# Recurrent core of a two-block kernel: where the first inverse products are put, and the order of the copies around them

## What is computed

```python
def step(state, inp):
    r_t, w_t, k_t, v_t, kk_t, a_t = inp
    sa = jnp.einsum('bhvk,bhk->bhv', state, kk_t)
    state = (state * w_t[:, :, None, :]
             - sa[..., :, None] * (kk_t * a_t)[..., None, :]
             + v_t[..., :, None] * k_t[..., None, :])
    return state, jnp.einsum('bhvk,bhk->bhv', state, r_t)
```

## Time and profile before

| | us |
|---|---|
| median of three executions | 2788.71 (2783.32 to 2795.54) |
| profiled execution, its time | 2797.66 |
| its span in the trace | 2795.9 |
| recurrent core, first copy of scores to last output product | 410.84 to 653.70 |
| PE busy in the whole span | 2590.9 (93%) |
| mean granted clock of TensorE | 0.954 |

### The profile page before, as it was taken

One profiled execution on the slowest core, in us unless ns is written; L12 is line 12 of the kernel. 1 busy time (PEld: TensorE's weight loads), 2 busy tenths in 40 slices (PEclk: granted clock), 3 DMA queues, 4 the chain that ended last, 5 costly groups with the idle time before them and its releaser, 6 DMA issues.

```text
span 2795.9 us, 35552 instructions
## 1 busy us (share of the span) xinstructions
PE 2590.9 (93%) x15475; PEld 1540.2 (55%) x15644; DVE 1138.2 (41%) x1288; ACT 561.5 (20%) x617; POOL 940.0 (34%) x390
## 2 busy tenths in 40 slices
PE   4869999999989999999998889999799999999996
PEld 1545558886445555555554556675345555555552
DVE  5466566663443220222224687355442220222233
ACT  3226431221121110011102323321231100111102
POOL 0212110000134444445545677201134443444450
PEclk7989999998989999999998999989899999999997
DMA  5432020000001111111113612300011111111101
GB/s 239 166 121 75 28 102 3 3 3 16 30 31 47 52 60 42 43 53 45 57 42 136 106 38 72 133 1 23 30 38 46 47 58 47 46 49 50 60 31 60
DMA packets 44267, 162.65 MB, mean 58 GB/s; under 512 B 4560, under 2 KB 14288, under 8 KB 41168
## 3 DMA queue, kind: packets, MB, share of 16 engines
q1 hardware_dynamic: 38496, 151.21, 16.3%
q10 hardware_dynamic: 5616, 9.17, 1.1%
HBM read 147.77 MB, written 12.58 MB: 57 GB/s over the span
## 4 chain that ended last, share of the span: by engine, by line
PE 86%; DVE 6%; issue 2%; DMA 2%; POOL 2%; ACT 1%; ACTq 0%; SPq 0%; DVEq 0%; POOLq 0%
PE pt L918 18%; PE pt L924 17%; PE pt L921 16%; PE pt L1233 11%; PE pt L561 7%; PE pt L411 3%; PE pt L700 2%; PE pt L1939 2%; PE pt L1945 2%; PE pt L1942 2%; PE pt L344 1%; DVE work L532 1%; DMA work<-in_xT 1%; PE pt L332 1%; PE pt L397 1%
## 5 line engine op out<-in xcount | busy, mean ns | idle before, releaser
L889 POOL TENSOR_TENSOR weights_rounded<-work,cst 128x1024 fp32r<-128x1024 f32 (+1 forms) x120 | 314.8, 2624 | 950.5 <-issue 683.8
L893 POOL TENSOR_TENSOR slots<-work,weights_rounded 128x1024 bf16<-128x1024 f32 (+1 forms) x120 | 346.3, 2885 | 9.4
L921 PE MATMUL pt<-work,weights_rounded 128*128 128x512 bf16 x1358 | 340.3, 382 | 2.8 <-issue 0.2
L561 PE MATMUL pt<-work 64*64 64x64 f32 (+5 forms) x4512 | 220.5, 250 | 13.4 <-DVE work L532 12.4
L921 PEld LDWEIGHTS pt<-work,weights_rounded 128*128 128x128 bf16 x1408 | 125.2, 99 | 182.2 <-issue 64.3
L561 PEld LDWEIGHTS pt<-work 64*64 64x64 f32 (+3 forms) x4512 | 202.2, 148 | 32.0 <-DVE work L532 17.3
L918 PE MATMUL pt<-rounded,weights_rounded 128*128 128x512 f32 x704 | 206.1, 428 | 8.8 <-DVE work L1859 5.2
L918 PE MATMUL pt<-rhs_rounded,weights_rounded 128*128 128x512 f32 x704 | 206.4, 429 | 7.8 <-DVE work L815 4.2
L918 PE MATMUL pt<-hidden_rounded,weights_rounded 128*128 128x512 f32 x704 | 207.5, 427 | 0.0
L1006 DVE SCALAR_TENSOR_TENSOR slots<-pt,par,slots 128x1023 f32<-128x1023 f32 x44 | 56.4, 1283 | 332.2 <-ACT slots L992 332.2
L924 PE MATMUL pt<-hidden_rounded,slots 128*128 128x512 bf16 x696 | 178.7, 387 | 1.0
(11 more groups left out here) (332 smaller groups left out, 3504.8 us busy)
## 6 DMA issues: line engine op xcount, KB each, us to landing
work<-in_w_up SPq DMA_DIRECT2D x88, 512.0 KB, 3.6
work<-in_w_mod SPq DMA_DIRECT2D x11, 2048.0 KB, 9.7
work<-in_w_down SPq DMA_DIRECT2D x32, 704.0 KB, 4.0
slots<-in_w_in SPq DMA_DIRECT2D x31, 512.0 KB, 4.1
slots<-in_w_v SPq DMA_DIRECT2D x10, 512.0 KB, 3.9
work<-in_xT ACTq DMA_DIRECT2D x4, 1024.0 KB, 22.8
x_scratch<-work SPq DMA_DIRECT2D x8, 512.0 KB, 2.7
slots<-in_w_out SPq DMA_DIRECT2D x8, 512.0 KB, 3.3
```

The source lines that it names most:

```text
L561: return pe.matmul(out, lhs, rhs, start=start, stop=stop, skip_group_check=True)
L889: did(pool, pool.tensor_tensor(w_hi(n, cols).rearrange("p (k n) -> p k n", n=P), w_raw(n, cols).rearrange("p (k n) -> p k n", n=P), const( ...
L893: did(pool, pool.tensor_tensor(w_lo(n, cols), w_raw(n, cols), w_hi(n, cols).bitcast(F32), ALU.subtract), "ffn_w_split")
L921: pe.matmul(out, top_half(w_hi(n, cols))[:, k * P:k * P + P], rhs_lo(k), start=False, stop=False, skip_group_check=True)
```

## The change

The first inverse products of pair `i` go to `PT[(i + 3) % 4]`: pair 0 to `PT[3]`, pair 1 to `PT[0]`, pair 2 to `PT[1]`. So they wait not for their own scores to be copied but for those of the pair before them, and those of pair 0 for none. `mv_kept` of the chunk before is now waited for ahead of them. DVE's order becomes: scores 0, scores 1, first inverse 0, scores 2, first inverse 1, first inverse 2. The mv products wait for first inverse 0 (their tile holds the products that it reads) and, pair by pair, for the copy of the scores. The X products of the first level wait one first inverse further, since their bank holds the products of the next pair. The order of the four quadrants in the first inverse products changes too. The number of instructions is the same.

```diff
+        def l_of(i):
+
+            return PT[(i + 3) % 4][:, :]
...
-                for i in range(3):
+                def scores_copy(i):
                     dve.wait_ge(E("products_done"), 3 * c + i + 1)
                     V_(dve.copy_predicated(heads(w(CA[i])), per_head(keep[:, 0:512], 512), heads(PT[i][:, :])), "scores_kept")
-                for i in range(3):
+
+                def first_inverse(i):
                     dve.wait_ge(E("inverse_unit"), 3 * c + i + 1)
                     dve.wait_ge(E("l_done"), 3 * c + i + 1)
-                    V_(dve.copy_predicated(heads(inverse(i)), per_head(keep[:, 512:640], P), heads(PT[i][:, :])[:, :, 0:P]),
+                    V_(dve.copy_predicated(heads(inverse(i)), per_head(keep[:, 512:640], P), heads(l_of(i))[:, :, 0:P]),
                        "inverse_ready")
+
+                scores_copy(0)
+                scores_copy(1)
+                first_inverse(0)
+                scores_copy(2)
+                first_inverse(1)
+                first_inverse(2)
...
-                for i in range(3):
-                    pe.wait_ge(E("scores_kept"), 3 * c + i + 1)
-                    for x, (left, right) in enumerate(((Z + i, B + i), (B + i, Z + i))):
-                        for q in range(2):
-                            for h in range(2):
-                                at = h * 512 + x * 64
-                                ins = mm(PT[i][half(q), at:at + 64], w(left)[half(h), tok[q]], w(right)[half(h), tok[q]])
-                    ins.then_inc(E("l_done"), 1)
                 if c > 0:
                     pe.wait_ge(E("mv_kept"), c)
                 for i in range(3):
+                    if i > 0:
+                        pe.wait_ge(E("scores_kept"), 3 * c + i)
+                    for x, (left, right) in enumerate(((Z + i, B + i), (B + i, Z + i))):
+                        for h, q in ((0, 0), (1, 1), (0, 1), (1, 0)):
+                            at = h * 512 + x * 64
+                            ins = mm(l_of(i)[half(q), at:at + 64], w(left)[half(h), tok[q]], w(right)[half(h), tok[q]])
+                    ins.then_inc(E("l_done"), 1)
+                pe.wait_ge(E("inverse_ready"), 18 * c + 1)
+                for i in range(3):
+                    pe.wait_ge(E("scores_kept"), 3 * c + i + 1)
                     for h in range(2):
                         ins = mm(PT[3][:, i * P + h * 64:i * P + h * 64 + 64], scores(i, h, 2), seqmaj(i, 3, h))
                 ins.then_inc(E("mv_done"), 1)
                 for n in range(5):
                     for i in range(3):
-                        pe.wait_ge(E("inverse_ready"), 18 * c + 3 * n + i + 1)
+                        pe.wait_ge(E("inverse_ready"), 18 * c + 3 * n + (min(i + 1, 2) if n == 0 else i) + 1)
```

## The result

| | before | after |
|---|---|---|
| median of 8 executions each, us | 2789.71 (2783.32 to 2800.42) | 2774.76 (2769.18 to 2779.29) |
| profiled execution, its time | 2797.66 | 2770.89 |
| its span | 2795.9 | 2769.1 |
| core, first copy of scores to the product behind the core | 242.86 | 224.82 |
| chunks of the core with a fall of the clock | 5 of 8 | 1 of 8 |

The ratio after to before is 0.9940, with a 95% interval of 0.9922 to 0.9958: 0.6% less time, 16.7 us of 2789.71 (11.7 to 21.8). The medians alone lie 15.0 us apart. The forecast was 2771 and a saving of 17.3.

What follows compares the result with a forecast made beforehand. The prediction took the serial front of each chunk (DVE copies, PE, DVE) and PE's lowered clock as the bound. A shorter path of 6.8 us plus 10.5 us of clock made 17.3, off 2788.7 to 2771, range 2762 to 2786.

Steps and rivals of the forecast that it cites:

- The bound: From first copy to first mask a chunk runs serially, DVE, PE, DVE; PE's work and its clock both matter.
- 0.85 us a chunk at full clock: Front of each chunk: T products start at 5.94 instead of 6.79 us; over eight chunks 6.8 us saved.
- a wait that did not hold: First level: X 1's new wait for first inverse 2 limits the gain to 0.85 of the mask's 0.94 us.
- hand-overs: DVE to PE ahead of last mv pair and X 0: 0.04 us each taken, 0.33 the costly bound.
- The clock, 10.5 us: Core: one fall of PE's clock left of five, saving 13.1 less 2.6 us; ends 13.1 and 0.
- The rule that spoke against it: Skill's rule: PE pausing briefly between groups swings between its clocks; by it the clock's 10.5 us would be 0.
- the starved stretch: PE's waits beside the score copies, 0.69 and 0.87 us with 0.46 us of work between, standing before the clock falls.
- the 0.20 us of the earlier trace: Pause in each level of full-speed chunks at clock 1.00, taken as partial evidence against the skill's rule.
- The clock falls as often as now: Rival: PE's thinned but longer stretch still lowers the clock; only 6.8 us saved, 2782 us, chance 0.22.
- The chunk does not get shorter: Rival: three hand-overs at mv of pair 2, X 0 and X 1 eat the 0.85; 2778 us, chance 0.09.
- Slower: Rival: the thin stretch at 2.3 to 5.4 us lowers the clock in every chunk; 2792 us, chance 0.07.
- From the profiled execution or from the median: Base of the forecast: 17.3 taken off the median 2788.7, giving 2771, not off the profiled 2797.66, giving 2780.4.

Runs made afterwards that it cites:

- first filler kernel: Kernel before with unused matmuls added in PE's two waits of a chunk, order and tiles unchanged: 2780.76 against 2791.21 us, ratio 0.9965.

## Why the prediction held, point by point

**The bound.** That DVE's copies and PE's work behind them are serial was read from the earlier trace rows. It stands: taking half the copy away shortened the chunk (28.14 to 27.53), while work added to PE in the waits did not lengthen it (28.95 in the first filler kernel).

**0.85 us a chunk at full clock.** Measured 0.80. The steps, in time from the first copy's start: first inverse 0 ends at 3.12 (forecast 3.11), mv of pairs 0 and 1 beside the third copy, last mv from 4.50 (4.46), first mask at 5.65 (5.51), first addition at 6.80 (7.60 less 0.85 is 6.75). The first mask came 0.14 late, most of it because mv of pair 2 took 0.59 us on PE (from 4.50 to 5.09) where 0.50 was taken. That cost only 0.05 at the addition, since the forecast had T waiting for X 1 and X 2, not for the mask. In the run the mask is last after all: T starts 0.06 us behind the end of the first mask in both kernels (6.80 before, 6.00 after), the mask and the chunk are both 0.80 us earlier, and the wait of X 1 for first inverse 2 adds nothing to that. X 1 and X 2 are through just ahead of it, so the two limits nearly meet. The forecast had taken 0.09 off for a wait that did not hold, and the mask came 0.14 late: two errors that left 0.05, by luck. The hand-overs cost 0.02 to 0.04 us in the chain, the value taken, and not the 0.33 of the upper end. Leaving DVE's order out of the change loses all of it (29.03 us), leaving the tile out and setting mv between the bursts loses half (28.52). That all three parts are needed is not shown, since PE's order was never changed alone.

**The clock, 10.5 us.** Measured from the chunks of the first traces: 18.0 in the core, less 8 x 0.80 = 6.4, leaves 11.6. Two things were off and nearly cancelled out in this term, so its agreement is in part luck. A fall that is left costs 1.3 to 1.5 us instead of the 2.6 taken from the old chunks, the clock being up again sooner, within about 4 us in the rows above. And the kernel before does not always lose 13.1: in the kernel with only the quadrants changed the core was 3.8 us shorter, which leaves 9.3. With the means of two traces each (240.96 and 225.52 us) the core's gain is 15.4, so the clock's share is 9.0. The first filler kernel, which gains by the clock alone, saved 9.8 us of the whole time. One and two falls were seen where one was assumed. PE's waits at the front of a chunk came to 0.68 us (0.46 and 0.22) where 0.9 was forecast.

**The rule that spoke against it.** The Trainium skill, "TensorE: Matmul & The Clock Gate", section "A second HAM failure mode: psum-queue depth-cycling", would have left the falls in place. The runs agree only in part: brief waits do bring a fall now and then (one and two chunks of eight), but less than the starved stretch (five of eight in two traces), and with fillers none. One reading that the prediction set against the rule was wrong. The 0.20 us of the earlier trace rows is DVE's idle time ahead of an addition. PE's weight loads pause 0.16 us there, and its MATMULs hardly at all (busy 1.98 of 2.00 us):

```profile
512.32 1.21 PEld L561 LDWEIGHTS pt<-work 64*64 64x64 f32 x35 [0.16 <-DVE work L546]
```

```profile
514.00:516.00 2.00, 1.98 (x62) 1.80 (x59) 1.65 (x6) 0.00 (x0) 0.00 (x0) 1.00 0.02 4
```

So the levels say little on what brief pauses of PE do.

**The rivals.** "The clock falls as often as now" is out by the chunk rows. "The chunk does not get shorter" is out by 28.14. "Slower" did not come about; its mechanism is nearest to the kernel with DVE's order only, where waits of 1.34 us and a longer path gave 1.0017.

**From the profiled execution or from the median.** Taking the saving off the median and not off the profiled execution was right: of the 26.8 us between the two profiled executions some 9 lie outside the core.

## What to carry to other kernels

Where an engine waits for a row of copies, look which consumer needs only the first results, and move its work beside the rest of the row; a tile that is free at that time can make it legal. Count the waits of TensorE twice, once on the path and once for the clock that they bring down afterwards: here the second price was the larger (some 9 to 12 us against 6.4), and matmuls without use, placed in the waits, earned it alone. Test the parts of such a change singly, every one of them: DVE's order and the quadrants alone, and the tiles with DVE's old order, gained nothing or lost here, and the one part that was not tried alone, PE's order, may be the one that carries the path.

## What the runs showed of the hardware that was not expected

One fp32 matmul of 128x128 by 128 columns, put between two bursts of 64x64 quadrant products, costs more than behind a product of its own kind. In the first filler kernel, behind the one of 256 columns with the same weights, its two records start 0.11 us apart (500.10 and 500.21). Between the bursts they start 0.21 us apart (469.28 and 469.49), the second burst follows at 469.70, and the first of the two starts only 0.17 us behind the start of the last product before it, where the products follow each other in about 0.06. So the second burst starts at 2.35 us of the chunk (469.70 less 467.35), although in the kernel after even the weights of both bursts are loaded by 2.09 (496.45 and 0.56, less 494.92). The kernel with mv between the bursts may suffer from the same: 28.52 us where 28.3 was expected. That wasn't tested by itself.

A fall of the clock has no fixed price, but it has two sizes. In all ten traces, read in stretches of half a microsecond, every fall in the core kept the lower level for either some 6.8 or some 3.4 us. This is one of the long ones, in the second chunk of before, to be set beside the short one of after that stands above:

```profile
446.00:448.00 2.00, 2.00 (x28) 1.88 (x29) 0.31 (x2) 0.49 (x1) 0.00 (x0) 0.50 0.00 0
448.00:450.00 2.00, 2.00 (x42) 2.00 (x40) 0.99 (x3) 0.00 (x0) 0.00 (x0) 0.50 0.03 8
450.00:452.00 2.00, 2.00 (x42) 2.00 (x42) 1.31 (x4) 0.00 (x0) 0.00 (x0) 0.50 0.00 0
```

The long ones cost 2.4 to 2.9 us a chunk and the short ones 1.1 to 1.5. All five in the trace of before are long; with only the quadrants changed two are long and three short; in the kernel after and with mv between the bursts all are short. In the four kernels that keep PE waiting longest (before, quadrants, DVE's order only, tiles only) the falls up to 5.09 us into the chunk were long and those from 5.12 us on short. The time in the chunk can't be the whole of it, for with mv between the bursts a fall at 4.8 us was short. Why some are long wasn't tested.
